# Two products of an inverse side by side in the matrix array, stores from another queue, and a last product in column groups

## What is computed

```python
h = _rms(x, norm_gain) * (1 + scale) + shift
qkv, z_a, beta, alpha, q, ckv, kr, z_b, g_a, g_b = split(h @ w_in)
# gated delta rule, 64-row chunks: tinv = (I + L)^-1 per head
o_a, s_new = _deltanet(qkv, beta, alpha, ...)
o_b = _mla(q, ckv, kr, ...)
merged = sigmoid(g_a) * ((o_a * silu(z_a)) @ w_o_dn) \
       + sigmoid(g_b) * ((o_b * silu(z_b)) @ w_o_mla)
y = x + gate * (merged @ w_out)
```

## Time and profile before

| | |
|---|---|
| median of 3 runs | 1830.23 us |
| the profiled execution's own time | 1830.37 us |
| its span on the core | 1828.6 us |
| mean granted TensorE clock | 0.985 |
| PE busy | 1749.6 us (96%) |
| DVE, ACT, POOL busy | 917.5, 642.5, 248.2 us |
| DMA | 284.06 MB, 155 GB/s in the mean |

### The profile page before, as it was taken

One profiled execution on the slowest core, in us unless ns is written; L12 is line 12 of the kernel. 1 busy time (PEld: TensorE's weight loads), 2 busy tenths in 40 slices (PEclk: granted clock), 3 DMA queues, 4 the chain that ended last, 5 costly groups with the idle time before them and its releaser, 6 DMA issues.

```text
span 1828.6 us, 28757 instructions
## 1 busy us (share of the span) xinstructions
PE 1749.6 (96%) x11174; PEld 1630.8 (89%) x11174; DVE 917.5 (50%) x1708; ACT 642.5 (35%) x1188; POOL 248.2 (14%) x353
## 2 busy tenths in 40 slices
PE   4899999999999899999999999989999998999998
PEld 2899999999999899999999978877888997999987
DVE  4544555754564876785223154454444445553442
ACT  4522524544443432323333243244333454021110
POOL 0111111213210701323111100000000121000000
PEclk7999999999999999999999999999999997999999
DMA  9222234678877744347454230033242897551322
GB/s 337 77 83 81 98 110 144 205 230 244 264 218 211 233 153 148 110 154 253 138 186 154 106 100 23 29 127 93 81 159 61 322 309 248 199 183 59 116 92 75
DMA packets 233394, 284.06 MB, mean 155 GB/s; under 512 B 43057, under 2 KB 190798, under 8 KB 233132
## 3 DMA queue, kind: packets, MB, share of 16 engines
q1 hardware_dynamic: 232940, 282.14, 48.3%
q10 hardware_dynamic: 160, 0.06, 0.0%
q0 software_dynamic: 160, 0.05, 0.0%
HBM read 177.30 MB, written 104.92 MB: 154 GB/s over the span
## 4 chain that ended last, share of the span: by engine, by line
PE 65%; issue 14%; POOLq 4%; DVE 4%; DMA 4%; POOL 2%; ACT 1%; SPq 1%; DVEq 1%; ACTq 0%
PE PS L2124 26%; PE PS L1000 10%; PE PS L415 7%; PE PS L1095 5%; PE PS L622 4%; PE PS L597 3%; PE PS L1210 2%; DMA ZA<-scratch_proj 2%; PE PS L610 2%; POOLq L1771 1%; POOLq L1718 1%; POOLq L1716 1%; PE PS L599 1%; PE PS L598 1%; DMA R<-scratch_gcum 1%
## 5 line engine op out<-in xcount | busy, mean ns | idle before, releaser
L2124 PE MATMUL PS<-HH,WL 128*128 128x352 f32 (+1 forms) x1728 | 384.5, 330 | 0.0
L2124 PE MATMUL PS<-HH,WH 128*128 128x352 f32 (+1 forms) x1728 | 372.4, 323 | 0.0
L2124 PE MATMUL PS<-HL,WH 128*128 128x352 f32 (+1 forms) x1728 | 371.7, 323 | 0.0
L2124 PEld LDWEIGHTS PS<-HH,WH 128*128 128x128 f32 (+1 forms) x1728 | 295.5, 187 | 0.3
L2124 PEld LDWEIGHTS PS<-HL,WH 128*128 128x128 f32 (+1 forms) x1728 | 292.9, 188 | 0.2
L2124 PEld LDWEIGHTS PS<-HH,WL 128*128 128x128 f32 (+1 forms) x1728 | 287.7, 189 | 2.9
L2246 DVE TENSOR_TENSOR WL<-Wraw,WH 128x2048 fp32r<-128x2048 f32 (+1 forms) x37 | 86.1, 2327 | 89.5 <-ACT WH L1840 88.3
L2259 DVE SCALAR_TENSOR_TENSOR R<-R,colA 128x1059 f32<-128x1059 f32 x72 | 97.2, 1350 | 5.5
L1860 ACT ACTIVATE R<-PS 128x1056 f32<-128x1056 f32 (+1 forms) x49 | 51.5, 1051 | 132.1 <-PE PS L2124 131.9
L647 ACT ACTIVATE pr<-PS,amx 128x128 f32<-128x128 f32 (+8 forms) x72 | 51.5, 715 | 131.7 <-DVE amx L681 131.7
L622 PE MATMUL PS<-V,pT 128*128 128x128 f32 (+1 forms) x624 | 86.2, 281 | 3.2 <-ACT pT L659 2.8
(11 more groups left out here) (332 smaller groups left out, 2901.7 us busy)
## 6 DMA issues: line engine op xcount, KB each, us to landing
scratch_proj<-R SPq DMA_DIRECT2D x72, 576.0 KB, 3.3
Wraw<-in_w_in SPq DMA_DIRECT2D x36, 1024.0 KB, 7.0
job<-scratch_proj SPq DMA_DIRECT2D x18, 512.0 KB, 6.3
fr<-scratch_u SPq DMA_DIRECT2D x16, 528.0 KB, 5.7
gr<-scratch_proj SPq DMA_DIRECT2D x16, 528.0 KB, 3.7
job<-scratch_proj SPq DMA_DIRECT2D x9, 768.0 KB, 7.4
Wraw<-in_w_ada SPq DMA_DIRECT2D x6, 1024.0 KB, 9.6
R<-scratch_gcum SPq DMA_DIRECT2D x9, 512.0 KB, 6.4
```

Of the source, the lines that this page charges most:

```text
L2124: last = pe.matmul(PS[0:m, 3 * (p % 2) + b, 0:TB], w[:, u % 2, k, j * P:j * P + m], x[:, k, b * TB:(b + 1) * TB], start=(k == 0 and first) ...
```

## The change

Four parts, with no change of what is computed.

1. **Transposes at the start.** From n = 16 on, the groups take banks 3, 4, 6 and 7 in turn, wait for the group four before (or the 15th), and stand earlier in PE's order.
2. **The inverse.** f3 of tile t - 1 joins f2 of tile t in one job: 8 + 8 products alternate, the one from partitions 0 to 63 into 64 to 127, the other from 64 to 127 into 0 to 63. 24 jobs become 17. The store of tile t - 1 and the load of tile t + 1 follow f2 of tile t.
3. **Delta.** `store_u` of tiles 0 to 6 is issued by ACT, after the squares; SP keeps the last two.
4. **Last product of y.** The sample rows are multiplied once in float32, in four column groups of 32: group c makes output columns 256 c to 256 c + 255. Two quarters of `w_out` are still in `Vraw`, two are loaded again (`wraw`). DVE makes four gate products of 32 partitions and one addition of 128, x and y of the sample move in four DMAs each.

```diff
+    def x_bank(n):
+        return 6 + n % 2 if n < 16 else (3, 4, 6, 7)[n % 4]
...
             if n >= 2:
-                pe.wait_ge(s_hf, n - 1)
+                pe.wait_ge(s_hf, n - 1 if n < 16 else max(n - 3, 15))
...
-        for k, tiles in zip(range(2, KD), ((16,), (17,), (18, 19), (20, 21), (22, 23), ())):
+        for n in range(16, 18):
+            x_back(n)
+        for k, tiles in zip(range(2, KD), ((18, 19), (20, 21), (22,), (23,), (), ())):
             first_chunk(k)
...
     for t in range(NT):
-        for i in range(3):
-            side[at(F0 + 3 * t + i)] = (f"f{i + 1}", t)
+        side[at(F0 + 3 * t)] = ("f1", t)
+        side[at(F0 + 3 * t + 1)] = ("f2", t)
+    side[at(F0 + 3 * NT - 1)] = ("f2", NT)
...
-                if kind == "f3":
-                    inverse_out(t)
-                    if t + 2 < NT:
-                        inverse_in(t + 2)
+                if kind == "f2" and t:
+                    inverse_out(t - 1)
+                    if t + 1 < NT:
+                        inverse_in(t + 1)
...
             for h in range(H):
-                x = pe.matmul(PS[HB:P, 7, h * HB:(h + 1) * HB], N21[t % 2][:, h], A1[:, h], start=True, stop=True)
-        if kind == "f3":
-            for h in range(H):
-                x = pe.matmul(PS[0:HB, 6, h * HB:(h + 1) * HB], Pm[:, h], XTs[t % 2][HB:P, h, HB:P], start=True, stop=True)
+                if t < NT:
+                    x = pe.matmul(PS[HB:P, 7, h * HB:(h + 1) * HB], N21[t % 2][:, h], A1[:, h], start=True, stop=True)
+                if t:
+                    x = pe.matmul(PS[0:HB, 6, h * HB:(h + 1) * HB], Pm[:, h], XTs[(t - 1) % 2][HB:P, h, HB:P], start=True, stop=True)
...
         for t in range(NT + 1):
-            if t == 2:
-                for g in range(2):
-                    sp.wait_ge(s_us[g], Z_OF_B)
             if t >= 2:
-                store_u(t - 2)
                 load_gate(t)
...
             x.then_inc(s_os, 1)
+            if t == 2:
+                for g in range(2):
+                    act.wait_ge(s_us[g], Z_OF_B)
+            if t >= 2:
+                store_u(act, t - 2)
...
-        store_u(NT - 1)
+        for g in range(2):
+            sp.wait_ge(s_us[g], Z_OF_B + 32 * (4 - g))
+        store_u(sp, NT - 1)
...
-        body(NT, 0)
+        for i in range(2):
+            pe.wait_ge(s_vr[i], 16 * (KD // 2 + 3))
+        pe.wait_ge(s_y, 2 * NT - 2)
+        for k in range(KD):
+            for c in range(4):
+                last = pe.matmul(PS[DEC * c:DEC * c + DEC, 0, 0:256], M4[:, k, SEQ:TOK], (wraw, Vraw)[c // 2][:, c % 2, k],
+                                 start=(k == 0), stop=(k == KD - 1), skip_group_check=True)
+        last.then_inc(s_yp, 1)
...
-        body(NT, 0, DEC, False)
+        dve.wait_ge(s_yp, NT + 3)
+        dve.wait_ge(s_xt[0], 16 * (NT // 2 + 4))
+        dve.wait_ge(s_ys[0], 16 * (NT // 2))
+        parts = [slice(DEC * c, DEC * c + DEC) for c in range(4)]
+        for c, r in enumerate(parts):
+            dve.tensor_tensor(yt[r, 0, 0:256], PS[r, 0, 0:256], gate[r, 1, 256 * c:256 * c + 256], ALU.mult)
+        dve.drain()
+        dve.tensor_tensor(yt[:, 0, 0:256], yt[:, 0, 0:256], xt[:, 0, 0:256], ALU.add).then_inc(s_y, 2)
...
-        sp.dma_start(o["y_sample"][0], yt[0:DEC, 0]).then_inc(s_ys[0], 16)
+        for c in range(4):
+            sp.dma_start(o["y_sample"][0, :, 256 * c:256 * c + 256], yt[DEC * c:DEC * c + DEC, 0, 0:256]).then_inc(s_ys[0], 16)
```

More of the change, by code:

```diff
@@ L1019, in sp_y @@
             sp_w_out(sp, i)
+        sp.wait_ge(s_o, 2 * KD)
+        sp.wait_ge(s_vlo, KD + 4)
+        for i in range(2):
+            sp.dma_start(wraw[:, i], a["w_out"][0, :, 256 * i:256 * i + 256].rearrange("(k p) n -> p k n", p=P)).then_inc(s_vr[i], 16)
         def store(t, s):
@@ L1055, in act_y @@
         tile(NT - 1, 1, P)
-        tile(NT, 0, DEC)
     def dve_y(dve):
@@ L1065, in body @@
         def body(t, slot, n, first):
-            if not (isinstance(t, int) and t in (0, NT)):
-                dve_low(dve, t + 1, 1 - slot, every, DEC if isinstance(t, int) and t == NT - 1 else P)
+            if not (isinstance(t, int) and t in (0, NT - 1)):
+                dve_low(dve, t + 1, 1 - slot, every, P)
             dve.wait_ge(s_yp, t + 3)
@@ L1074, in body @@
                         dve.wait_ge(s_ys[slot], 16 * ((t - slot) // 2))
-                g = 1 if isinstance(t, int) and t == NT else 0
-                dve.tensor_tensor(yt[0:n, slot, c], PS[0:n, 4 * slot + h], gate[0:n, g, c], ALU.mult)
+                dve.tensor_tensor(yt[0:n, slot, c], PS[0:n, 4 * slot + h], gate[0:n, 0, c], ALU.mult)
                 dve.drain()
@@ L1129, in load_delta, with store_u @@
             sp.dma_start(tile3(d[0:n, b])[:, :, 0:n], tile3(scr[name][t, 0:n])[:, :, 0:n]).then_inc(s_dl[t % NSL], 16)
+    def store_u(eng, t):
+        n = rows_of(t)
+        for g in range(2):
+            eng.wait_ge(s_u2, 2 * t + g + 1)
+            eng.dma_start(scr["u"][4 * g:4 * g + 4, :, t * P:t * P + n].rearrange("c p n -> p c n"),
+                          UA[:, t % 2, g].rearrange("p (h n) -> p h n", h=4)[:, :, 0:n]).then_inc(s_us[t % 2], 16)
     def sp_delta(sp):
@@ L1556, in inverse_out @@
         def inverse_out(t):
-            sp.wait_ge(s_sr, turns["f3", t] + 1)
+            sp.wait_ge(s_sr, turns["f2", t + 1] + 1)
             sp.dma_start(scr["xt"][t], XTs[t % 2].rearrange("p h n -> p (h n)")).then_inc(s_fs[t % 2], 16)
@@ L1898, in act_pass01 @@
             gain, shift = G[:, k, g // 2:g // 2 + 1], mod[:, k, g // 2:g // 2 + 1]
-            x = act.activation(hf[:, n % NHF, 0:w], PS[:, 6 + n % 2, 0:w], ACT.Identity, scale=gain, bias=shift)
+            x = act.activation(hf[:, n % NHF, 0:w], PS[:, x_bank(n), 0:w], ACT.Identity, scale=gain, bias=shift)
             if g != 1:
-                x = act.activation(HH[:, k, cols], PS[:, 6 + n % 2, 0:w], ACT.Identity, scale=gain, bias=shift)
+                x = act.activation(HH[:, k, cols], PS[:, x_bank(n), 0:w], ACT.Identity, scale=gain, bias=shift)
             x.then_inc(s_hf, 1)
@@ L2000, in act_side @@
         if kind == "f2":
-            act.activation(Pm, PS[HB:P, 7].rearrange("p (h n) -> p h n", h=H), ACT.Copy).then_inc(s_sr, 1)
-        if kind == "f3":
-            act.wait_ge(s_xi, 2)
-            act.activation(XTs[t % 2][0:HB, :, HB:P], PS[0:HB, 6].rearrange("p (h n) -> p h n", h=H), ACT.Copy).then_inc(s_sr, 1)
+            if t < NT:
+                x = act.activation(Pm, PS[HB:P, 7].rearrange("p (h n) -> p h n", h=H), ACT.Copy)
+            if t:
+                act.wait_ge(s_xi, 2)
+                x = act.activation(XTs[(t - 1) % 2][0:HB, :, HB:P], PS[0:HB, 6].rearrange("p (h n) -> p h n", h=H), ACT.Copy)
+            x.then_inc(s_sr, 1)
     def act_decay(act, step):
@@ L2060, in x_back @@
             if n >= 2:
-                pe.wait_ge(s_hf, n - 1)
+                pe.wait_ge(s_hf, n - 1 if n < 16 else max(n - 3, 15))
             for t in range(4 if g < 2 else 1):
                 r = P if g < 2 else DEC
-                last = pe.transpose(PS[:, 6 + n % 2, t * P:t * P + r], R[0:r, 4 * g + t, k * P:(k + 1) * P], ident[0:r, 0:r])
+                last = pe.transpose(PS[:, x_bank(n), t * P:t * P + r], R[0:r, 4 * g + t, k * P:(k + 1) * P], ident[0:r, 0:r])
             last.then_inc(s_xT, 1)
```

17 lines of the change are left out of this document (7 added, 10 removed).

## The result

| | before | changed |
|---|---|---|
| median (range) | 1829.88 us (1828.25 to 1831.47), 4 runs | 1810.88 us (1808.85 to 1814.28), 4 runs |
| ratio | | 0.9898 [0.9883, 0.9913] |
| profiled execution / span | 1830.37 / 1828.6 us | 1814.28 / 1812.5 us |

The changed kernel is faster by 1.02%, 19.0 us, where the forecast (1812.0 us) was 18.2 us. The profiled execution happens to be the slowest of the four; its mean granted clock (1 is full clock, 2.4 GHz; 0.5 is half clock, 1.2 GHz) is 0.981, that of the other three 0.986 and 0.987. So the trace has to be read piece by piece, with what half clock takes beside each piece.

What follows compares the result with a forecast made beforehand. PE, busy nine tenths of the span, was taken as the bound, with the DMA engines bounding delta. Gains of 3.7 + 5.9 + 2.0 + 6.6 = 18.2 us from 1830.2 gave 1812.0 us, range 1806.5 to 1823.

Steps and rivals of the forecast that it cites:

- start: Start: PE runs through without its 2.07 us wait, projection begins at 65.2 us for 68.84: 3.7 us gained.
- inverse: Inverse: seven joint jobs save 7.0 us with a ninth lost in overlap, less a 1.1 us wait: 5.9 us gained.
- delta: Delta: store issues leave SP, so output projection weights and last u rows are requested sooner: 2.0 us gained.
- last product: End of y: product in four column groups takes 4.0 us for 11.05; with DVE and store issues, 6.6 us gained.
- the store lands at about 981, the loads at 985.3 ... PE waits 1.1 us: Inverse, store issued at 971.37 us behind large transfers: f1, due at 984.2 us, waits 1.1 us for its loads.
- where the queue runs dry towards the end: Late delta: SP's store issues (1.27 and 1.03 us) stand on the chain; removing them gains about 2.0 us.
- I count nothing: Delta's stretch with full DMA engines: fewer SP store issues only let loads queue up sooner, no gain counted.
- (d): Rival, delta: ACT's store issues are held as SP's are, ACT 29 us late, time 1841 us; 5%.
- (e): Rival, delta: a milder hold of ACT's issues, a pair some 6 us, within 0.2% of no change; 3%.
- (a): Rival, inverse: corners don't overlap, gain 0.6 us instead of 5.9, time 1817.3 us; 15%.
- (b): Rival, delta: ACT's stores delay the gate loads, 3.9 us lost instead of 2.0 won, time 1817.9 us; 15%.
- (c): Rival, last product: column groups don't overlap, 14.2 us instead of 4.0, time 1822.2 us; 5%.

Runs made afterwards that it cites:

- p1_again: The kernel before with only the start changed (four banks, earlier transposes), measured a second time: 1828.21 us, ratio 0.9981 to the kernel before.
- c1: The changed kernel with all second products ahead of all third products in each joint job of the inverse: 1816.71 us, ratio 0.9913 to the kernel before.
- c2: The changed kernel with the last product going through its column groups one after the other: 1819.45 us, ratio 0.9928 to the kernel before.
- c3: The changed kernel with SP issuing a finished inverse tile's store and next loads ahead of weights and q: 1807.31 us, ratio 0.9860 to the kernel before.
- v1: The changed kernel with c3's order, one DVE gate pass at the end and two last stores issued by ACT: 1802.69 us, ratio 0.9836 to the kernel before.
- a0: The changed kernel unaltered, measured once more beside others on one chip: 1811.61 us, ratio 0.9898 to the kernel before.
- s1: The changed kernel with the four banks kept but the last transpose groups at their old places: 1816.54 us, ratio 0.9908 to the kernel before.
- c4: The changed kernel with delta's stores of u issued by SP again, behind the same step's loads: 1819.59 us, ratio 0.9924 to the kernel before.
- p2: The kernel before with only the inverse's joint jobs and the transfers that hang on them: 1828.44 us, ratio 0.9979 to the kernel before.
- p3: The kernel before with only delta's stores issued by ACT: 1827.15 us, ratio 0.9973 to the kernel before.

## Why the prediction was right

The time was right to 1.1 us. The terms one by one:

| term | forecast | traces | alone, by ratio |
|---|---|---|---|
| start | 3.7 us | 3.4 at full clock, 1.8 to 2.3 with half clock in it (2.2 in the changed kernel's) | 2.2 (two series) |
| inverse | 5.9 us | 4.5 (8.8 less the wait and half clock) | 3.8 |
| delta | 2.0 us | 4.5 to y | 4.9 |
| last product | 6.6 us | 7.1 | 8.2 |
| sum | 18.2 us | 18.3 | 19.1 |

The changed kernel's span is shorter by only 16.1 us: 0.7 us more came from before the changed part of the start, but the projection ahead of the inverse was 1.1 us slower, and the latents and attention 1.8 us.

**The start** went as its steps say. Five traces with the earlier places (p1_again, c1, c2, c3, v1) have full clock there, and all go from the transpose of the modulation's columns to the projection in 12.1 us, where before it was 15.5 us (the columns' transpose stood at 53.34 us): 3.4 us, 0.3 less than forecast.

**The inverse** was right in its mechanism and wrong in two sizes that partly cancel. The ninth lost to imperfect overlap, carried over from the column groups, isn't there: two corners overlap wholly, and 8.8 us took the place of 7.0. The Trainium skill's rule ("TensorEngine Tiling (Array Packing)", Key Properties) that tiles run in parallel was the better guide, and the traces agree with it: 0.029 us an instruction on two corners, 0.06 to 0.067 on one. The step that failed is "the store lands at about 981, the loads at 985.3 ... PE waits 1.1 us": the place was right and the size was not. It let the store start once the engines were free, as in the kernel before, where the weights went out 8.2 us ahead of it. Now they go out 2.0 us ahead of it [the rows at 964.08 and 966.04]. So the store itself sat 4.34 us in SP, and the loads behind it waited for its landing. The wait was 2.7 us in this trace, 1.3 to 3.7 us in the others with this order. And no term had the half clock that follows a wait: 980 to 984 us at 0.57 costs 0.43 x 4 = 1.7 us more. 8.8 - 2.7 - 1.7 = 4.4, against 4.5 seen. The same sum comes out within 0.1 us in a0, s1, c2, c4 and, with its 5.3, c1, and within 0.7 in p2.

**Delta** was under-sized, and the mechanism was right. The step that failed is the size of the term "where the queue runs dry towards the end", 2.0 us from the issues of the stores alone, 1.27 and 1.03 us. Between the loads of the last tile and the weights `Vraw`, three pairs of stores and three gate loads had stood in SP. Without the stores the gate loads too went out in 0.37 to 0.61 us each, where the last had taken 2.79. The rows of u were asked for 5.2 us sooner and `Vraw` 5.4, which is the upper end that was given (5 us). "I count nothing" for the full stretch was nearly right: the gate loads queued up sooner and landed 2.0 us later, at the same time and 1.3 us sooner. In the eight traces with ACT's stores the fifth gating comes 64.7 to 65.7 us after the stage's first product, in the five without 65.9 to 67.3; `Vraw` is asked for at 75.4 to 76.4 us and at 78.8 to 81.8. PE's waits within delta were 2.69, 0.43 and 2.82 us and are 1.41, 0.60, 0.48 and 1.29.

ACT's issues cost 0.37 to 0.55 us in this trace and 0.89 at most in the others, near the forecast's 0.5. That refutes (d) and (e), both of which rested on SP's held issues. The Trainium skill's page "DMA: Bandwidth & Descriptors" (Issuing engines are not separate DMA queues) leaves only the issuing time to be saved. The trace agrees in the main: of the full stretch's gate loads only the fifth landed sooner, by 1.3 us, and the rest of the 5.4 is issuing time, but some 4 us of it and not 2.

**The last product** went as forecast: 3.6 us for it where 4.0 stood, DVE 1.81 + 0.42 = 2.2 us for 2.0, four store issues 1.72 us for 1.6. From tile 7's end to the span's end it is 9.2 us for 9.6.

**The rivals**: (a) is refuted by the corners' 0.029 us, (b) by p3's 4.9 us (a gate load did land 2.0 us later, once, and that was made up by the fifth), (c) by 3.6 us where it gave 14.2, (d) and (e) by ACT's issue times. That the sum came so near is in part luck: the start was 1.5 us too high, the inverse 1.4 (2.1 by its own run) and delta 2.5 (2.9) too low. The bound "two of four terms under half their size" was not reached by any.

## What to carry over

Small products that use a corner or a strip of the array should be woven together instruction by instruction with others on free parts: as neighbours they cost a half or less than a third, in blocks next to nothing is won (0.06 us an instruction for 0.067 on a corner). When a job moves in the order of work, write down what stands ahead of its transfers in the issuing engine's queue at the new place; a store in front of a load chain belongs ahead of bulk loads that have slack. Stores that wait for results belong on the queue of an engine that isn't feeding the loads. But when the DMA engines are full, count a load by when it lands: with its issue over 7.7 us sooner it landed no sooner.

## What was not expected of the hardware

- By the records, PE starts instructions past others that were issued earlier, where these wait for an occupied part of the array (898.38 us in c1, 1810.47 us in c2: three were passed each time).
- **Half clock after a wait.** The granted clock falls to 0.5 for some 3.5 us after a wait of PE, though not always. Of the kernels with the inverse's wait, after, p2, c1, c2 and c4 (2.7 to 3.7 us) show it at 980 to 988 us, p2 for twice as long; a0 and s1 (1.6 and 1.3 us) don't. At the start the wait of 1.24 us near 50 us is in all kernels: with the earlier places the half clock came at 52 to 57 us in four traces of nine. Without them it never came there, but in three traces of five at 66 to 71 us, behind the wait of 2.07 us. Whether the earlier places draw it forward is left open.
- In the changed kernel's trace another stretch, at 1052 us, makes up nearly all of the 1.8 us lost where the diff changes nothing. It follows the wait of 1.74 us ahead of the chunks' first product, which all fourteen traces have. From that product to attention it takes 135.4 us, as c2 does, whose clock fell at 1056 us; the twelve other traces take 133.8 or 133.9. One stretch costs about 1.7 us, as much as a term of the sum. Near 636 us every trace has one or two in a row (the clock over 628 to 646 us is 0.91 in four, 0.81 or 0.82 in ten). Stretches that come or stay away may be why single runs of one kernel differ by 5 us and more; no run isolates that.
- A DVE pass of 32 rows and 256 columns takes 0.43 us, as long as one of 128 rows (0.42): four of them for one was the price that the column groups put on the end, and v1 had it back.
